# Keys of the memory attention transposed by way of DRAM and VectorE instead of TensorE

## What is computed

```python
def memory_attention(q, mem, mem_norm_g, w_mem_kv, q_norm_g, k_norm_g):
    B, M, _ = mem.shape
    kv = rms_norm(mem, mem_norm_g) @ w_mem_kv
    k, v = jnp.split(kv.reshape(B, M, 2 * MEM_HEADS, HEAD_DIM), 2, axis=2)
    q = rms_norm(q, q_norm_g)
    k = rms_norm(k, k_norm_g)
    logits = jnp.einsum('bshd,bmhd->bhsm', q, k).astype(jnp.float32) * (HEAD_DIM ** -0.5)
    p = jax.nn.softmax(logits, axis=-1)
    out = jnp.einsum('bhsm,bmhd->bshd', p.astype(v.dtype), v)
    return out.reshape(B, q.shape[1], MEM_WIDTH)
```

## Time and profile before

| | |
|---|---|
| median of 3 executions | 912.81 us (912.79 to 912.90) |
| profiled execution: own time | 912.87 us |
| profiled execution: span, first to last instruction | 910.8 us |
| TensorE clock granted | 1.00 of full speed (2.4 GHz) in all 40 slices |
| busy: PE, DVE, ACT, POOL | 905.8, 635.5, 501.3, 107.2 us |
| DMA | 168.26 MB, mean 185 GB/s |

### The profile page before, as it was taken

The page is one execution under the profiler, slowest core; times in us unless marked ns, Lnnn a source line. Parts: engine busy times, 40 slices in busy tenths (PEclk is TensorE's granted clock), DMA queues, the critical chain, the costliest instruction groups (busy, mean ns, idle before and its releaser), DMA issues.

```text
span 910.8 us, 15058 instructions
## 1 busy us (share of the span) xinstructions
PE 905.8 (99%) x4998; PEld 769.0 (84%) x4998; DVE 635.5 (70%) x970; ACT 501.3 (55%) x750; POOL 107.2 (12%) x186
## 2 busy tenths in 40 slices
PE   9999999999999999999999999999999999999998
PEld 6888888888888888888888888888888788888887
DVE  6766577687677766566778766656878776666665
ACT  6654455565655554454564645445676664545542
POOL 2052302003000000000002930000121000000000
PEclk9999999999999999999999999999999999999999
DMA  9897656556346656565375865665443276566551
GB/s 294 268 278 231 196 187 183 186 157 212 88 141 201 213 173 201 184 194 195 119 213 164 265 199 173 208 185 185 141 137 117 76 243 214 183 206 188 171 171 47
DMA packets 140195, 168.26 MB, mean 185 GB/s; under 512 B 12488, under 2 KB 104624, under 8 KB 140160
## 3 DMA queue, kind: packets, MB, share of 16 engines
q1 hardware_dynamic: 135616, 164.67, 56.9%
q0 software_dynamic: 4368, 3.07, 1.6%
q10 hardware_dynamic: 176, 0.07, 0.0%
HBM read 166.19 MB, written 1.05 MB: 184 GB/s over the span
## 4 chain that ended last, share of the span: by engine, by line
PE 99%; DVE 1%; ACT 0%; issue 0%; POOL 0%; ACTq 0%; POOLq 0%
PE ps L1763 35%; PE ps L1768 18%; PE ps L1977 8%; PE ps L1975 8%; PE ps L1973 8%; PE ps L1849 5%; PE ps L1851 5%; PE ps L1850 5%; PE ps L1733 1%; PE ps L2101 1%; PE ps L1802 1%; PE ps L2182 1%; PE ps L2070 0%; PE ps L1816 0%; PE ps L2139 0%; PE ps L2236 0%
## 5 line engine op out<-in xcount | busy, mean ns | idle before, releaser
L1763 PE MATMUL ps<-mainT,w_hi 128*128 128x512 f32 x1376 | 468.7, 393 | 0.2
L1148 DVE TENSOR_TENSOR w_lo<-w_raw,w_hi 128x1024 fp32r<-128x1024 f32 x296 | 350.7, 1221 | 42.6 <-ACT w_hi L739 42.2
L1768 PE MATMUL ps<-mainT,w_lo 128*128 128x256 f32 x1376 | 350.5, 280 | 0.0
L739 ACT CAST w_hi<-w_raw 128x1024 fp32r<-128x1024 f32 x296 | 299.7, 1047 | 28.3 <-PE ps L1763 11.2
L1763 PEld LDWEIGHTS ps<-mainT,w_hi 128*128 128x128 f32 x1376 | 248.9, 188 | 46.2 <-issue 0.5
L1768 PEld LDWEIGHTS ps<-mainT,w_lo 128*128 128x128 f32 x1376 | 255.8, 189 | 13.8
L797 ACT COPY gate_up_f<-ps 128x512 f32<-128x512 f32 x88 | 51.2, 582 | 105.0 <-PE ps L1763 99.6
L1240 DVE TENSOR_TENSOR gate_up_f<-ps,gate_up_f 128x256 f32<-128x256 f32 x88 | 37.2, 423 | 90.5 <-ACT gate_up_f L797 90.4
L1977 PE MATMUL ps<-w_hi,actT_lo 128*128 128x512 f32 x320 | 98.9, 390 | 0.0
L1975 PE MATMUL ps<-w_lo,actT_hi 128*128 128x512 f32 x320 | 98.9, 390 | 0.0
L1973 PE MATMUL ps<-w_hi,actT_hi 128*128 128x512 f32 x320 | 98.6, 389 | 0.0
(11 more groups left out here) (248 smaller groups left out, 844.0 us busy)
## 6 DMA issues: line engine op xcount, KB each, us to landing
w_raw<-in_ffn_w_gate_up_dram SPq DMA_DIRECT2D x352, 256.0 KB, 3.9
w_raw<-in_ffn_w_down_dram SPq DMA_DIRECT2D x176, 256.0 KB, 3.5
w_raw<-in_w_in_dram SPq DMA_DIRECT2D x32, 256.0 KB, 3.5
w_raw<-in_w_out_dram SPq DMA_DIRECT2D x32, 256.0 KB, 3.4
w_raw<-in_w_mem_kv_dram SPq DMA_DIRECT2D x16, 256.0 KB, 3.0
w_raw<-in_w_kv_dram SPq DMA_DIRECT2D x8, 256.0 KB, 3.5
ycat<-in_mem_dram SPq DMA_DIRECT2D x1, 1024.0 KB, 7.5
z<-in_mem_dram POOLq DMA_DIRECT2D x32, 32.0 KB, 4.1
```

Of the source, the lines that this page charges most:

```text
L739: ins = nc.scalar.copy(half(w_hi[s], b), half(w_raw[s], b))
L1148: ins = nc.vector.tensor_tensor(half(w_lo[s], b), half(w_raw[s], b), half(w_hi[s], b).bitcast(F32), ALU.subtract)
L1763: return pe.matmul(gate_sums(fb, j)[:, :, tokens], w_hi[units[k // 4][0]][:, k % 4, cols], both[:, k, :, tokens], start=start, stop=stop)
L1768: return pe.matmul(gate_sums(fb, j)[:, 0, tokens], w_lo[units[k // 4][0]][:, k % 4, cols], both[:, k, 0, tokens], start=False, stop=False)
```

## The change

PE no longer transposes the keys of either layer. Once `head_scale` is done, POOL writes the scaled keys (256 KB) to a DRAM tensor `mk_rows`, waits until they have landed, and reads them back with four DMAs, one for each block of 32 of the 128 partitions (64 KB each, in pieces of 32 floats = 128 bytes). DVE turns the result in 32x32 blocks (`memory_key_turns`), and ACT copies it from SBUF to `mkT` with the norm vector multiplied in (`memory_key_copy`). The staging tiles are free parts of `z` (layer 0) and of `shared` (layer 1). In layer 1 DVE's `head_sums("mk1")` moves ahead of `probs_copy(2)`, and ACT's copy moves from behind `query_squares(1, 0)` to behind the split of Y1's second row tile. PE waits for `headT_ready` ahead of the scores of round 5, no longer ahead of the turn of the query.

```diff
@@ gpsimd
+            def memory_key_blocks(l):
+
+                pool.wait_ge(head_ready, HEADREADY.index(f"mk{l}") + 1)
+                pool.dma_start(mk_rows[l].rearrange("(t p) c -> p t c", p=P),
+                               mkv_sb[:, :, 0:MEMH * HD]).then_inc(mk_rows_landed, 16)
+                pool.wait_ge(mk_rows_landed, 16 * (l + 1))
+                keys = mk_rows[l].rearrange("(i f) (n q c) -> q f n i c", f=BLOCK, q=BLOCKS, c=BLOCK)
+                blocks = mk_blocks[l].rearrange("p (n i c) -> p n i c", n=MEMH // 2, c=BLOCK)
+                for q in range(BLOCKS):
+                    pool.dma_start(blocks[q * BLOCK:(q + 1) * BLOCK, :, :, :], keys[q]).then_inc(mk_blocks_landed, 16)
+
             head_roots("mk0")
+            memory_key_blocks(0)
             pool.wait_ge(consts_landed, 16 * SMALL_LOADS)
...
             head_roots("mk1")
+            memory_key_blocks(1)
             head_roots(("qm1", 0))
@@ scalar
+            def memory_key_copy(l):
+
+                act.wait_ge(mk_blocks_turned, l + 1)
+                g = 3 * l
+                nc.scalar.activation(mkT[:, :, :].rearrange("p n t -> p (n t)"), mk_turned[l], ACT.Copy,
                                      scale=head_gain_col[:, g:g + 1]).then_inc(headT_ready, 1)
...
-            head_copy(0)
-            head_copy(1)
+            memory_query_copy()
+            memory_key_copy(0)
             z_copy(0, 0, 0)
...
             query_squares(1, 0)
-            head_copy(2)
             split("Y1", 0, 0)
             high_unit("out1", 1)
             query_copy(1, 0)
             split("Y1", 1, 0)
+            memory_key_copy(1)
             z_copy(1, 1, 1)
@@ vector
+            def memory_key_turns(l):
+
+                dve.wait_ge(mk_blocks_landed, 16 * BLOCKS * (l + 1))
+                nc.vector.transpose(mk_turned[l], mk_blocks[l]).then_inc(mk_blocks_turned, 1)
...
-            low_unit("out0", 0)
+            low_unit("out0", 0, (0,))
+            memory_key_turns(0)
+            low_unit("out0", 0, (1,))
             maxima(0)
...
             low_unit("z1b", 1)
-            probs_copy(2)
             dve.wait_ge(mkv_ready, 2 * NT)
             head_sums("mk1")
+            probs_copy(2)
             head_scale("mk1").then_inc(head_ready, 1)
...
             low_unit("out1", 0, (1,))
+            memory_key_turns(1)
             maxima(4)
@@ tensor
                 if k == 3:
                     pe.wait_ge(mkv_ready, NT)
-                    turn_heads(0)
-                elif k == 6:
-                    turn_heads(1)
+                    turn_memory_queries()
...
                     values(2)
-                    turn_heads(2)
...
                     values(3)
-                    pe.wait_ge(headT_ready, 4)
+                    pe.wait_ge(mkv_ready, 2 * NT)
                     turn_query(1, 0)
...
             scores(4)
+            pe.wait_ge(headT_ready, 4)
             scores(5)
```

More of the change, by code:

```diff
@@ L132 @@
 HEADREADY = ["mk0", "k1", "mk1"]
-HEADTS = [("mq0", 7, 1), ("mk0", 6, 0), ("mk1", 1, 3)]
+MQ_BANK = 7
 QUERIES = [(0, 0), (0, 1), (1, 0), (1, 1)]
@@ L237, in encoder_kernel @@
         mkT = sb("mkT", [P, MEMH // 2, S])
+        mk_rows = [nc.dram_tensor(f"mk_rows{l}", [S, MEMH * HD], F32, kind="Internal").ap() for l in range(2)]
         mqT = sb("mqT", [P, MEMH // 2, S])
@@ L244, in encoder_kernel @@
         qT = shared[:, 0:8 * S].rearrange("p (n t) -> p n t", n=8)
+        mk_blocks = [z[:, 0, 0:512], shared[:, 8 * S:8 * S + 512]]
+        mk_turned = [z[:, 1, 0:512], shared[:, 8 * S + 512:8 * S + 1024]]
         probs = sb("probs", [P, 2, SOFT])
@@ L286, in encoder_kernel @@
         keys_landed = sem("keys_landed")
+        mk_rows_landed = sem("mk_rows_landed")
+        mk_blocks_landed = sem("mk_blocks_landed")
+        mk_blocks_turned = sem("mk_blocks_turned")
         consts_landed = sem("consts_landed")
@@ L910, in ffn, with memory_query_copy @@
                     split(into, 1, 1)
[L912 to L920, removed]
+            def memory_query_copy():
+                act.wait_ge(consts_landed, 16 * SMALL_LOADS)
+                act.wait_ge(ones_ready, 5)
+                act.wait_ge(head_turned, 1)
+                nc.scalar.activation(mqT[:, :, :].rearrange("p n t -> p (n t)"), ps[:, MQ_BANK, :], ACT.Copy,
+                                     scale=head_gain_col[:, 1:2]).then_inc(headT_ready, 1)
+            def memory_key_copy(l):
+                act.wait_ge(mk_blocks_turned, l + 1)
+                g = 3 * l
+                nc.scalar.activation(mkT[:, :, :].rearrange("p n t -> p (n t)"), mk_turned[l], ACT.Copy,
                                      scale=head_gain_col[:, g:g + 1]).then_inc(headT_ready, 1)
@@ L2033, in ffn, with turn_memory_queries @@
                 end_bank(1, 1)
[L2035 to L2042, removed]
+            def turn_memory_queries():
+                pe.wait_ge(z_ready, NT)
+                v = head_view("mq0")
                 for n in range(2):
                     for t in range(NT):
-                        mm = pe.transpose(ps[:, bank, (n * NT + t) * P:(n * NT + t + 1) * P],
+                        mm = pe.transpose(ps[:, MQ_BANK, (n * NT + t) * P:(n * NT + t + 1) * P],
                                           v[:, t, 2 * n:2 * n + 2, :].rearrange("p n d -> p (n d)"), ident[:, :])
```

## The result

| | before | after |
|---|---|---|
| median of 20 executions each | 912.79 us (912.54 to 912.99) | 914.05 us (913.46 to 915.58) |
| ratio, 95% interval | | 1.0015 (1.0009 to 1.0022) |
| profiled execution: own time, span | 912.87, 910.8 us | 914.79, 913.0 us |
| TensorE clock granted | 1.00 | 1.00 |
| HBM written | 1.05 MB | 1.57 MB |

The time is inside the predicted range, and by the 0.2% that counts as a difference here it is no change. But the interval lies wholly above 1: the change costs 1.3 us where 0.2 were forecast, and the new kernel scatters over 2.1 us where the old one scatters over 0.45. Both the missing microsecond and the scatter are what the experiments are about.

The account below looks back on a forecast made before the run. PE bounds the kernel, holding 99% of the chain. Layer 0 nets -0.44 + 0.2 = -0.24, layer 1 -0.42 + 0.85 = +0.43: +0.19 on 912.87 gives 913.06, median 913.0 us, no change; range 912.0 to 915.5.

Parts of the forecast that it names:

- Removed, 0.86: PE's transposes of the keys gone: 0.44 us gained in layer 0 and 0.42 in layer 1, the whole gain found.
- steps 1 to 4: Layer 0: keys scaled at 213.27, write landed at 215.85, last of four reads issued at 217.7, landed at 221.3.
- Steps 5 and 6: Layer 0: DVE's turn done at 222.05, ACT's copy at 222.8; PE, there at 222.80, stalls 0.2 us.
- The rule against the rows: Skill page's estimate: write 2.6 us, 64 KB read 2.15; blocks there by 219.9, no layer 0 stall, sum 912.8.
- a stall of 0.85: Layer 1: ACT's copy, queued behind the split of Y1, makes PE wait 0.85 us before round 5's scores; net +0.43.
- 0.8 us to spare: Layer 1: blocks land at 687.3, before DVE reaches the turn at 688.13, so DVE finds them landed.
- the forecast's own signs of being wrong: PE waiting over 2 us in layer 0, DVE waiting for layer 1's blocks, clock below 1.00, or a new later wait.
- What is queued behind the new waits: DVE's second weight half and maxima, POOL's casts and roots, SP's slot reuse: all stay hidden and cost nothing.
- blocks late in layer 0: Rival, chance 0.19: 128-byte pieces drain slowly beside out0's weights; blocks land at 223.4, PE stalls 2.3 us, time 915.1.

Follow-up runs that it names:

- l1_only: Layer 1 goes the new way, layer 0 stays as in the kernel before; 913.00 us, ratio 1.0001.
- hold: Changed kernel, but SP holds back the loads of out0's second to fourth unit until layer 0's blocks have landed; 912.91 us, ratio 1.0002.
- early_rows: Changed kernel, but both DRAM writes move to 149.4 and 150.2 us and hold memory-token columns, leaving only the reads on the path; 912.80 us, ratio 0.9999.
- defer5: Changed kernel, but PE does two chunks of the next product before the scores of round 5; ACT's order stays; 913.78 us, ratio 1.0012.
- wide: Changed kernel, but the four reads fetch the same bytes in 2 KB pieces, leaving keys in wrong places; 913.66 us, ratio 1.0010.
- l0_only: Layer 0 goes the new way, layer 1 stays as in the kernel before; 913.81 us, ratio 1.0011.
- hold2: Changed kernel, but only out0's third and fourth unit loads are held back; the second unit's loads still meet the write; 913.94 us, ratio 1.0009.
- act_reads: Changed kernel, but ACT's queue instead of POOL's issues the four reads of both layers; the write stays on POOL; 915.63 us, ratio 1.0028.
- all: Changed kernel with `act_reads`, `hold` and `defer5` joined; 913.93 us, ratio 1.0011.
- hold_defer: Changed kernel with `hold` and `defer5` joined, all reads issued by POOL; 912.27 us, ratio 0.9994.
- sp_reads: As `hold_defer`, but SP issues two of layer 0's four reads; 912.81 us, ratio 1.0001.

## Why the prediction was right, and where it was off

The verdict, no change, and the range were right, and so was the structure: a gain of 0.86 us eaten by two waits of PE for `mkT`, at the two places named. The sum was +0.19 and the measurement is +1.26 (+1.4 inside the span), because of one term. That the own time came out no further off is in part luck: 0.3 us were given back outside the span, of which the forecast knew nothing.

- **Removed, 0.86.** Right. In layer 0 the stretch from the product ahead of the turn to the last one ahead of the scores took 1.82 us before (221.09 to 222.91) and 1.37 after (221.21 to 222.58), 0.45 less; the turn's place in layer 1 is 0.37 to 0.4 us shorter.
- **Layer 0, steps 1 to 4: a stall of 0.2, in the trace 1.90.** This is the step that failed, in its sizes. Scaling ended a little earlier than planned (0.69 us instead of 1.08 for the multiplication; the two traces with POOL's casts beside it, before and `l1_only`, have 1.08, the others 0.69), and the write's issue started at 213.29 (planned 213.35). Then the write with POOL's taking up took 3.20 us instead of 2.55 (+0.65), the three issues 2.0 instead of 1.8 (+0.2), the last landing 4.8 instead of 3.6 (+1.2). Together 2.0 us: 223.28 instead of 221.3. The write had been priced from transfers in other stretches, with no look at the loads issued ahead of it (in before's trace the DMA share is 0.90 from 211 to 213 us and 0.36 from 213 to 216), and the read from the upper half of the earlier trace rows rather than its end, although showed the share at 0.75 there. `hold` shows that these loads are the cause: without them the write lands in 2.6, the reads in some 2.2, and the stall is 0.2. So the forecast held for a quiet stretch, and the stretch was not quiet. In the median execution the loss is about 0.7 us smaller than in this trace, by the two times. Steps 5 and 6 have a small error as well: with the blocks in time the stall was to be 0, and in `hold` and `early_rows`, where DVE does not wait, PE still comes 0.26 and 0.19 us late by starts. DVE turned at 221.4 to 221.5 and not at 221.13, as the first half of the weights or the multiplication ahead of it took longer than before (1.50 us instead of 1.2, 1.09 instead of 0.69).
- **The rule against the rows.** The Trainium skill, page "DMA: Bandwidth & Descriptors" (anatomy of one DMA, SWDGE path), has about 2.0 us and the bytes over the rate for one DMA. Its estimates, 2.6 and 2.15, are what `hold` measured, 2.6 and some 2.2. Beside other loads the traces disagree, with 2.9 to 4.2 for the write and up to 4.8 for a read, and the measurement decides.
- **Layer 1: a stall of 0.85, in the trace 1.00 by starts, 0.83 by the wait's own figure.** Right, and for the reason given: in `early_rows` the blocks are early and 0.6 remain (0.8 by starts); in `defer5` PE asks later and nothing remains. The blocks had no 0.8 us to spare, though, and DVE waiting for them was one of the forecast's own signs of being wrong. They were forecast for 687.3, with layer 0's 1.57 us on top for 688.9, and landed at 689.90: the write was issued 0.3 us later than that, the write with its taking up took 2.8 us instead of 2.5, the three issues 2.0 instead of 1.8, and the last landing 3.8 instead of 3.6. DVE was there at 689.6. It cost 0.2 us.
- **What is queued behind the new waits.** Right: the roots of the queries' heads ended on POOL at 223.8 instead of 221.3 and nobody waited for them or for DVE's second half. The clock stayed at 1.00, even behind PE's idle 1.84 us.
- **The rival "blocks late in layer 0".** Its effect came true in part (223.28 against its 223.4), its mechanism did not: `wide` has 2 KB pieces, and its landings in layer 0 are within those of the small pieces. It priced the time at 915.1; the scatter reaches 915.58, the median does not.

## What to carry to other kernels

A round trip through DRAM in front of the engine that bounds the kernel is two landings in series, and each must be priced with the loads around it, above all those that were issued before it. Here it was 2.6 and 2.2 us with the loads held back, 2.9 to 4.2 for the write and 2.3 to 4.8 for a read beside them; the DMA share tells a quiet stretch from a busy one, but not which landing a busy one will give. If the round trip must be there, hold other loads back for its time, and let its reader stand behind other work; the two edits together gave back 1.8 us of own time. Moving the reader has a price too (0.3 us here), and DVE's own order left 0.2, so that of 0.86 us taken out some 0.3 remained. A copy that moves from one engine's list to another place needs the same look: whatever stands ahead of it there decides, however early its data are.

## What the runs showed of the hardware

- The same 256 KB write to DRAM, from the same place in the program, landed in 2.6 us in the four traces with the loads held back and in 2.9 to 4.2 in the six with loads from 209 us on in flight; at 149 us, beside other loads, two of its size took 5.1 and 6.3 (`early_rows`).
- The range of an experiment's 8 to 11 executions went with that only loosely. It was 2.7 and 2.5 us in `l0_only` and `defer5` (2.1 in the 20 of after), but 1.0 to 1.6 in `hold2`, `act_reads` and `wide`, which have the write beside loads too. It was 0.5 in `l1_only` and `early_rows`, which have no write in this place, and 0.2, 0.75, 1.2 and 1.25 in `all`, `hold_defer`, `hold` and `sp_reads`, which hold the loads back; the last two have one long execution each.
- Issuing a 64 KB read in 512 pieces costs 0.70 us on POOL and 0.65 on ACT's and on SP's queue; in 2 KB pieces 0.50 on POOL. No queue was cheap, and on ACT the issue holds up the engine's own work.
- Pieces of 128 bytes and of 2 KB landed alike in the busy stretch of layer 0 (2.9 to 4.8 us in three traces, 3.2 to 4.2 in one), but not in layer 1, where the longest of four landings was 2.3 us with 2 KB (one trace) and 3.3 to 4.1 with 128 bytes; in `early_rows`, whose reads start 3 to 5 us sooner, it was 2.6.
- A multiplication of 128x512 on DVE took 0.69 us in most places, but 1.08 to 1.34 in four where POOL's casts ran beside it (before, `l1_only`, `early_rows`, `sp_reads`). It also took 1.15 in after, beside POOL's issues of the reads, where `l0_only` has 0.69 beside the same, so what lengthens it is not settled.
